# A two-layer attention block on one NeuronCore: filling work dealt out over three units of the next branch, a new order ahead of the attention, and gated outputs on GpSimd

## The reference, cut to what matters

```python
def merge_branches(o_m, o_s, o_a, z_m, z_s, z_a, g, lw):
    y_m = (o_m.reshape(B, T, MLA_WIDTH) * jax.nn.silu(z_m)) @ lw['w_o_mla']
    y_s = (o_s.reshape(B, T, SWA_WIDTH) * jax.nn.silu(z_s)) @ lw['w_o_swa']
    y_a = (o_a.reshape(B, T, AX_WIDTH) * jax.nn.silu(z_a)) @ lw['w_o_ax']
    y = jax.nn.sigmoid(g_m) * y_m + jax.nn.sigmoid(g_s) * y_s + jax.nn.sigmoid(g_a) * y_a
    return y @ lw['w_out']

def hybrid_layer(x, ctx, c, c_ctx, lw, pos, update_ctx):
    ...
    h = rmsnorm(x, lw['norm_w']) * (1 + scale) + shift
    p = h @ lw['w_in']
    k_m, v_m, k_s, v_s, k_a, v_a = project_kv(p[..., :KV_COLS], lw, pos)
    q_m, q_s, q_a, z_m, z_s, z_a, g = project_q(p[..., KV_COLS:], lw, pos)
    ...
    x = x + gate * merge_branches(o_m, o_s, o_a, z_m, z_s, z_a, g, lw)
```

## Time and profile before

| what | us |
|---|---|
| runs, median (lowest to highest) | 1764.51 (1763.14 to 1766.87) |
| the profiled execution, its own time | 1766.55 |
| its span | 1764.7 |
| PE busy | 1694.5 (96%) |
| PE weight loads busy | 1488.8 (84%) |
| DVE busy | 1081.5 (61%) |
| ACT busy | 1047.0 (59%) |
| POOL busy | 535.6 (30%) |
| mean granted clock of PE | 0.98 |

### The profile page before, as it was taken

The page is one execution under the profiler, slowest core; times in us unless marked ns, Lnnn a source line. Parts: engine busy times, 40 slices in busy tenths (PEclk is TensorE's granted clock), DMA queues, the critical chain, the costliest instruction groups (busy, mean ns, idle before and its releaser), DMA issues.

```text
span 1764.7 us, 26891 instructions
## 1 busy us (share of the span) xinstructions
PE 1694.5 (96%) x10496; PEld 1488.8 (84%) x10496; DVE 1081.5 (61%) x2188; ACT 1047.0 (59%) x1919; POOL 535.6 (30%) x306
## 2 busy tenths in 40 slices
PE   7999999999999999999999998999999999999997
PEld 3778888889989889899889986788888887888787
DVE  6534777765555656665774655567775656665634
ACT  3345777766666777765321254577766678777322
POOL 2432223222132211222322354333233333233442
PEclk8999999999999999999999999999999999999999
DMA  9111111111121111111635231112122221222642
GB/s 330 40 37 29 26 46 37 48 31 49 44 60 37 43 43 43 37 43 42 230 123 191 97 99 49 41 38 56 40 53 66 72 72 31 62 59 55 203 144 95
DMA packets 178530, 129.51 MB, mean 73 GB/s; under 512 B 21658, under 2 KB 167652, under 8 KB 178404
## 3 DMA queue, kind: packets, MB, share of 16 engines
q1 hardware_dynamic: 174240, 115.36, 22.8%
q10 hardware_dynamic: 2884, 8.24, 1.2%
q0 software_dynamic: 1280, 4.20, 0.7%
HBM read 123.58 MB, written 4.19 MB: 72 GB/s over the span
## 4 chain that ended last, share of the span: by engine, by line
PE 76%; DVE 10%; ACT 8%; issue 3%; POOL 2%; DMA 1%; SPq 0%; DVEq 0%; ACTq 0%; POOLq 0%
PE acc L1383 55%; PE wide L1435 6%; PE ptp L1455 6%; PE pv L1468 4%; PE pv L1469 3%; DVE nmax L2019 2%; ACT e L1702 2%; DVE pt L2044 1%; ACT w_hi L1620 1%; POOL h_lo L1871 1%; POOL w_lo L1826 1%; DVE k_s L1572 1%; DVE k_m L1572 1%; ACT k_m L1563 1%; DMA w_raw<-in_ada_w 1%
## 5 line engine op out<-in xcount | busy, mean ns | idle before, releaser
L1826 POOL TENSOR_TENSOR w_lo<-w_raw,w_hi 128x1024 fp32r<-128x1024 f32 (+2 forms) x192 | 392.5, 2047 | 1042.5 <-ACT w_hi L1620 1042.5
L1383 PE MATMUL acc<-h_hi,w_hi 128*128 128x512 f32 (+2 forms) x1320 | 465.5, 353 | 12.0 <-DVE cq_lo L1574 3.9
L1383 PE MATMUL acc<-h_hi,w_lo 128*128 128x512 f32 (+2 forms) x1320 | 463.9, 352 | 0.0
L1383 PE MATMUL acc<-h_lo,w_hi 128*128 128x512 f32 (+2 forms) x1320 | 458.7, 351 | 0.3 <-POOL h_lo L1871 0.3
L1383 PEld LDWEIGHTS acc<-h_hi,w_hi 128*128 128x128 f32 (+1 forms) x1320 | 249.6, 189 | 52.8 <-issue 8.9
L2019 DVE TENSOR_REDUCE nmax<-wide 128x1 f32<-128x768 f32 (+3 forms) x240 | 189.6, 790 | 170.4 <-PE wide L1435 168.8
L1717 ACT ACTIVATE pt<-ptp 128x512 fp32r<-128x512 f32 (+3 forms) x312 | 165.7, 563 | 213.2 <-PE ptp L1455 211.5
L1383 PEld LDWEIGHTS acc<-h_hi,w_lo 128*128 128x128 f32 (+1 forms) x1320 | 249.3, 189 | 33.4
L1383 PEld LDWEIGHTS acc<-h_lo,w_hi 128*128 128x128 f32 (+1 forms) x1320 | 246.6, 188 | 34.4 <-POOL h_lo L1871 0.5
L1709 ACT ACTIVATE e<-e,einv 128x768 f32<-128x768 f32 (+3 forms) x240 | 193.4, 806 | 68.1 <-DVE einv L2036 67.7
L2044 DVE TENSOR_TENSOR pt<-ptp,pt 128x512 fp32r<-128x512 f32 (+3 forms) x312 | 191.9, 640 | 44.4 <-ACT pt L1717 44.4
(11 more groups left out here) (217 smaller groups left out, 3074.7 us busy)
## 6 DMA issues: line engine op xcount, KB each, us to landing
w_raw<-in_w_in SPq DMA_DIRECT2D x102, 512.0 KB, 3.9
w_raw<-in_ada_w SPq DMA_DIRECT2D x48, 512.0 KB, 5.1
w_raw<-in_w_out SPq DMA_DIRECT2D x16, 512.0 KB, 3.8
w_raw<-in_w_in SPq DMA_DIRECT2D x16, 256.0 KB, 3.1
w_raw<-in_w_o_mla SPq DMA_DIRECT2D x16, 256.0 KB, 2.7
w_raw<-in_w_o_swa SPq DMA_DIRECT2D x16, 256.0 KB, 2.8
w_raw<-in_w_o_ax SPq DMA_DIRECT2D x16, 256.0 KB, 2.7
w_raw<-in_mla_w_uq SPq DMA_DIRECT2D x16, 144.0 KB, 2.3
```

The lines of the kernel that those rows point to most:

```text
L1383: ins = nc.tensor.matmul(dst, lhs, rhs, start=first, stop=last)
L1826: nc.gpsimd.tensor_tensor(w_lo[s][:, 0:k], w_raw[s][:, 0:k], f(w_hi[s][:, 0:k]), ALU.subtract).then_inc(w_lo_ready, 1)
```

## The change

It has seven parts.

1. `BEHIND = 3`: the filling work of a branch is dealt out over its units and three of the next branch. The first branch counts three units more, the last three fewer, and the branch for `fill` is that of unit i-3.
2. `ak`'s first group is deferred: its event `E` comes after row tile 1 is turned and modulated, not before.
3. The second `latent_sums` (context) comes before the query latents, not between them.
4. `KC` comes in `first_pair` behind the second group of values, and the groups there stand in another order; the z groups name another `oldest` chunk, which decides how soon later weights may be split.
5. The gating at `O` moves from DVE (a product with the factor 0.5) to POOL (a plain product, with waits for POOL's own earlier writes); the factor goes into the pieces `H` and `L` of og.
6. In `y` (for the second and third branch) and `wout`, DVE writes the product back into the PSUM bank and not to SBUF, and adds from there. A group that follows in this bank waits for the sum (`th_done`, `xr_done`) and not for the product.
7. swa's sum of the exponentials with the sink, one column, is a `tensor_scalar` with a column as scalar and not a `tensor_tensor`.

```diff
-DRAIN = 2
+DRAIN, BEHIND = 2, 3
...
-        left[BRANCHES[-1]] += DRAIN
+        left[BRANCHES[0]] += BEHIND
+        left[BRANCHES[-1]] += DRAIN - BEHIND
...
             if i < len(units) + DRAIN:
-                branch = u["branch"] if u else BRANCHES[-1]
+                branch = units[min(max(i - BEHIND, 0), len(units) - 1)]["branch"]
...
-        ak = project("ak", l, ck, "x", roped=True, oldest=ck, low_last=True, halves=True, parts=2)["steps"]
+        ak_x = project("ak", l, ck, "x", roped=True, oldest=ck, low_last=True, halves=True, parts=2, defer=True)
+        ak = ak_x["steps"]
         ckv = project("ckv", l, cks[0], "x", t=0, oldest=ck, halves=True, parts=2)["steps"]
         run_all([ak[0], ckv[0]])
         turn_rows(0)
         modulate_rows(0)
         run_all(ak[1:])
-        ropes_ak = n["rope"]
         turn_rows(1)
         modulate_rows(1)
+        ak_x["read"]()
+        ropes_ak = n["rope"]
         run_all(ckv[1:])
...
         latent_sums("x")
+        latent_sums("c")
         query_latents(0, "c")
         query_latents(1, "x")
-        latent_sums("c")
         query_latents(1, "c")
...
-        emit("KC", l_done=n["l"])
+        ropes_read = n["l"]
...
-            order = [keys_["x"], q0["x"], values[0], keys_["c"], q1["x"], values[1]]
-            order += [q0["c"], z["c"], q1["c"], z["x"]] if "c" in tgs else [z["x"]]
+            order = [keys_["x"], q0["x"], values[0], q1["x"], values[1], keys_["c"]]
+            order += [z["c"], q0["c"], q1["c"], z["x"]] if "c" in tgs else [z["x"]]
             for g in order:
                 go(g)
+                if g is values[1]:
+                    emit("KC", l_done=ropes_read)
...
-                        if before is not None and before["dve"] and before["kind"] not in ("statb", "statq"):
+                        if before is not None and before["kind"] == "wout":
+                            if new(xr_done, before["xr"]):
+                                pe.wait_ge(xr_done, before["xr"])
+                        elif before is not None and "th" in before:
+                            if new(th_done, before["th"]):
+                                pe.wait_ge(th_done, before["th"])
+                        elif before is not None and before["dve"] and before["kind"] not in ("statb", "statq"):
...
+                elif ev == "O":
+                    if new(o_sum, pa["o"] + 1):
+                        pool.wait_ge(o_sum, pa["o"] + 1)
...
+                    nc.gpsimd.tensor_tensor(o, o_half[own, 0:k], o, ALU.mult).then_inc(o_free, 1)
...
-                            nc.vector.scalar_tensor_tensor(t, t, 1.0, src[:, 0:N], ALU.add, ALU.mult).then_inc(acc_free, 1)
+                            nc.vector.scalar_tensor_tensor(src[:, 0:N], t, 1.0, src[:, 0:N], ALU.add, ALU.mult).then_inc(acc_free, 1)
...
-                            nc.vector.tensor_tensor(y, y, t, ALU.add).then_inc(th_done, 1)
+                            nc.vector.tensor_tensor(y, src[:, 0:N], y, ALU.add).then_inc(th_done, 1)
...
-                        nc.vector.tensor_tensor(x_add[:, :], src[:, 0:256], gate[:, s, c], ALU.mult).then_inc(acc_free, 1)
+                        nc.vector.tensor_tensor(src[:, 0:256], src[:, 0:256], gate[:, s, c], ALU.mult).then_inc(acc_free, 1)
...
-                        link(nc.vector.tensor_tensor(esink[:, r:r + 1], esink[:, r:r + 1], esum[:, r:r + 1], ALU.add))
+                        link(nc.vector.tensor_scalar(esink[:, r:r + 1], esum[:, r:r + 1], esink[:, r:r + 1], None, ALU.add))
...
-                    nc.vector.scalar_tensor_tensor(o, o_half[own, 0:k], 0.5, o, ALU.mult, ALU.mult).then_inc(o_free, 1)
```

More of the change, by code:

```diff
@@ L732, in first_pair @@
                               needs=lambda: latents, what="qm", head=1, **roped(tg)) for tg in tgs}
-            z = {tg: project("z", l, cz, tg, branch=BRANCHES[0], t=1, before_z=0, oldest=cq) for tg in tgs}
-            order = [keys_["x"], q0["x"], values[0], keys_["c"], q1["x"], values[1]]
-            order += [q0["c"], z["c"], q1["c"], z["x"]] if "c" in tgs else [z["x"]]
+            z = {tg: project("z", l, cz, tg, branch=BRANCHES[0], t=1, before_z=0, oldest=None if tg == "x" else c) for tg in tgs}
+            order = [keys_["x"], q0["x"], values[0], q1["x"], values[1], keys_["c"]]
+            order += [z["c"], q0["c"], q1["c"], z["x"]] if "c" in tgs else [z["x"]]
             for g in order:
                 go(g)
+                if g is values[1]:
+                    emit("KC", l_done=ropes_read)
             zs[BRANCHES[0], 1] = [z[tg] for tg in tgs]
@@ L997, in build @@
               for i in part]
-    a_row, x_add = shared("a_row", [4, D], F, 83968), shared("x_add", [P, 256], F, 49152)
+    a_row = shared("a_row", [4, D], F, 83968)
     xres = shared("xres", [P, TT, D], F, 100352)
@@ L1673, in _ @@
                             act.wait_ge(acc_done, g["acc"])
-                        ins = high_parts(*pieces(g, e["kv"]))
+                        hi, _, whole_o = pieces(g)[0][0]
+                        ins = nc.scalar.activation(hi, whole_o, ACT.Copy, scale=0.5)
                     elif g["kind"] == "kx":
@@ L1815, in _ @@
             new = counting()
-            link = splits = tiles = 0
+            link = splits = tiles = ropes = 0
             for e in events:
@@ L1858, in _ @@
                     link += 1
+                    ropes = g["rope"]
                     nc.gpsimd.tensor_tensor(swapped[rows, :], swapped[rows, :], sin[rows, :], ALU.mult).then_inc(rope_link, 1)
@@ L1865, in _ @@
                             pool.wait_ge(rope_done, g["rope"])
+                elif ev == "O":
+                    pa = e["pa"]
+                    own, _ = o_rows(pa)
+                    k = len(pa["units"]) * P
+                    if new(o_sum, pa["o"] + 1):
+                        pool.wait_ge(o_sum, pa["o"] + 1)
+                    if new(acc_free, pa["zs"]):
+                        pool.wait_ge(acc_free, pa["zs"])
+                    if new(w_lo_ready, splits):
+                        pool.wait_ge(w_lo_ready, splits)
+                    if new(rope_done, ropes):
+                        pool.wait_ge(rope_done, ropes)
+                    o = o_t[own, pa["h"] // 2, o_tokens(pa)]
+                    nc.gpsimd.tensor_tensor(o, o_half[own, 0:k], o, ALU.mult).then_inc(o_free, 1)
+                    if new(o_free, pa["o"] + 1):
+                        pool.wait_ge(o_free, pa["o"] + 1)
                 elif ev == "XM":
@@ L1999, in _ @@
                         x = xres[:, g["tt"], c]
-                        nc.vector.tensor_tensor(x, x, x_add[:, :], ALU.add).then_inc(xr_done, 1)
+                        nc.vector.tensor_tensor(x, src[:, 0:256], x, ALU.add).then_inc(xr_done, 1)
                 elif ev == "L":
@@ L2007, in _ @@
                         ins = nc.vector.scalar_tensor_tensor(y_lo[:, g["t"], c], y2[:, g["t"], c], 0.5, f(y_hi[:, g["t"], c]), ALU.mult, ALU.subtract)
+                    elif g["kind"] == "og":
+                        hi, lo, whole_o = pieces(g)[0][0]
+                        ins = nc.vector.scalar_tensor_tensor(lo, whole_o, 0.5, f(hi), ALU.mult, ALU.subtract)
                     else:
```

## The result

| | us |
|---|---|
| before, median (lowest to highest) | 1764.12 (1763.14 to 1766.87) |
| changed, median (lowest to highest) | 1778.69 (1772.46 to 1779.37) |
| ratio, 95% interval | 1.0075 (1.0062 to 1.0089) |
| forecast | 1757, range 1746 to 1767 |

The range missed by 12 us and the sign was wrong. The profiled execution took 1778.86 us, its span is 1777.1.

A forecast was written before the change was run, and what follows sets the result against it. PE was taken as the bound, 96% busy: its work, its waits and the slow clock behind them. Terms of 22.3 us off and 15.0 on gave 7.3 us less, from 1764.51 to 1757 us, range 1746 to 1767.

The forecast's parts named there:

- The two handovers of layer 1 get mla's and swa's own leftovers until the closing: Part 1, layer 1's branch handovers: filling removes waits of 2.5 and 3.0 us and slow clock, 9.5 us off.
- Its price is thinner filling in mla: Part 1, mla of both layers: less filling per unit becomes PE waiting, 4 us on, bounds 1 and 9.
- nothing there: Part 1, layer 0's handovers: filling already stands in every step, so no gain was counted.
- The handover to ax: Part 1, layer 1 at 1461 to 1467 us: the 3.0 us wait and 3.4 us of slow clock go.
- Parts 3 and 4: Latent sums, key copy and first pair's order, ahead of the attention: 2.3 and 5.4 us off.
- Part 7: swa's column sum: never above 217 ns, the wait near 372.5 us shrinks, 3.1 us off, bounds 0 and 4.
- Part 6: Sums out of PSUM: 0.5 us gained, 4.5 us lost as 11 groups in layer 0 wait for the bank.
- Part 2: ak deferred: second ckv tile waits 2.9 us in each layer, less h_lo waits, plus slow clock; 6.5 us on.
- Part 5: Gating on POOL instead of DVE: 1.5 us off, bounds -5 and 6.
- DVE's relief: Rival, mla: less DVE work shortens the way to PV, some 8 us more off, 1749 us; 17%.
- hold up the weights: Rival: gating on POOL makes w_lo late and PE waits; 1772 us with 20 of 120 passes; 9%.
- It comes out even: Rival: nothing may run at the handovers, or new waits bring twice the slow clock; 1764 us; 16%.

The follow-up runs named there:

- a_mla3: Changed kernel with the three units behind at the end of mla only, swa's filling over its own units: 1775.88 us, ratio 1.0064.
- a_swa3: Changed kernel with the three units behind at the end of swa only: 1757.67 us, ratio 0.9958.
- e_half: Changed kernel with part 1 undone, but mla's heads 0 to 3 thinned and the later heads making up for it: 1774.05 us, ratio 1.0056.
- e_late: Changed kernel with three units behind mla only, heads 0 to 3 dealt full and the second half thin: 1772.71 us, ratio 1.0045.
- b_esink: Kernel before with part 7 alone: 1759.11 us, ratio 0.9970.
- nb_ak: Changed kernel with parts 1 and 2 undone: 1757.45 us, ratio 0.9949.
- b_gate: Kernel before with part 5 alone, the gating on POOL: 1764.06 us, ratio 1.0003.

## Why the prediction was wrong

The step that failed is "The two handovers of layer 1 get mla's and swa's own leftovers until the closing", with "Its price is thinner filling in mla" at 4 us. In its place the runs show work for swa's first head made late and key pieces moved in front of `o_half`: 17 us for three units behind mla (a_mla3), nothing for three behind swa (a_swa3). Its sum was -9.5 + 4.0; part 1 measured +17 alone and +19 in the changed kernel. All other parts together were forecast at -1.8 and measured -5.6 (0.9968, with -3.5 to -7.8 by its interval). The miss is part 1 alone, and in it the units behind mla. By its steps:

- **That leftovers exist.** True for swa, false for mla. Each item that counts for mla in `queue` is used by mla or by swa's first head: its queries and keys at the first scores, its values at the first `PV`. `SA` and `PV` force them however little credit there is. I took the name in `of` for the branch that pays and did not ask who reads the item first. The list says it: `item((SWA, 0), "mla", ...)`. The empty place of layer 1 was filled all the same, because swa's own items start three units later and last until the outputs close. In exchange there is a burst ahead of swa's first scores in layer 1, two thin steps behind them, and PE waits up to 6.5 us for the query pieces, in one layer or both. The turn of layer 1 went from 6.3 us of idle time to 7.3, and to 5.2 with part 1 undone.
- **Layer 0's handovers: "nothing there".** There was nothing to gain, but something to lose: 8.6 us, more than in layer 1. A stretch without a wait was costed at nothing, though its cover was the 7.7 us by which the queries were early: now PE waits 2.9 us there, at a clock of 0.66 over 10 us.
- **4 us for thinner units.** In the changed kernel heads 0 to 3 lose 10.2 us and heads 4 to 6 give back 2.1, 8 in all, inside the bound of 9. But e_half, thin units alone, costs some 15 us, outside it, so the term was mis-sized as well, and how the 17 us divide between thinness and lateness stays open: e_half's 15 and e_late's 14 do not add up to them. The amount is not the cause alone. Filling comes in parts of some 0.9 us, so that 0.12 us less a unit means one part less in about every eighth unit, and from there on every other part stands in another step. Where such a step has few parts, or its pieces fill DVE, and it meets the close of a pass, PE waits: up to 2.1 us for `o_half` in the changed kernel, 4.4 in e_half and e_late. One, two and three units cost 16, 30 and 17 us.
- **The handover to ax.** The wait of 3.0 us and its slow clock are gone, as forecast; a wait of 2.7 us for a z reading and 0.83 over 10 us took its place.
- **Parts 3 and 4** were right: -7.7 forecast, -7.4 measured, with the wait for key pieces as forecast.
- **Part 7** was right in kind, short in size (-3.1 against -5.3, interval 3.0 to 7.6, bound 4). I counted one wait, where ten of the 80 sums took 0.4 us or more. By the same reckoning b_esink's trace has 2.9 us less idle time in layer 0's turn, where that wait lies, but also 1.2 us less in layer 1's turn and 1.7 in swa behind it.
- **Part 6**: +4.0 net forecast, +4.9 measured, with eight of the eleven waits in the list. The rule of the Trainium skill on a PSUM source (VectorE: DVE Perf Modes, The TRN2 errata), 62 cycles more than for one in SBUF, is not borne out here: the sum with its source in PSUM takes 0.69 us as it did from SBUF. DVE of the changed kernel at 709 us:

```profile
709.01 0.69 DVE L2000 SCALAR_TENSOR_TENSOR acc<-th_x,acc 128x512 f32<-128x512 f32 x1
709.73 0.69 DVE L2003 TENSOR_TENSOR y<-acc,y 128x512 f32<-128x512 f32 x1
```

- **Part 2**: the waits came as forecast, 2.5 us in the list (2.7 from the starts) against 2.9, in both layers. The chain of the forecast adds up to 60.4 us and not 60.6 (57.9 + 0.63 + 0.57 + 1.3), which gives 2.6 us of wait, as measured. The cost is nearer 3.4 than 6.5, since the waits net of `h_lo` were 2.5 us and not 3.1, and in the kernel that nb_ak is compared with the clock fell behind one of the two and not both (by the starts of the matmuls, 1.3 us of slow clock where 3.4 were counted).
- **Part 5**: -1.5 forecast, 0 measured, inside its error.
- **The rivals.** DVE's relief carried nowhere: in b_gate, 50 us less of it left mla's waits as they were (4.9 and 4.0 us in layer 0, against 4.4 and 3.9). POOL did not hold up the weights: PE's matmuls wait 2.8 us in all for `w_lo` in b_gate and in the kernel before. "It comes out even" came nearest, yet its mechanism (nothing may run at the handovers) gives 0, not a loss. No rival had the loss that came: an item needed soon made later. The range was too narrow on the slow side besides. The slow bounds of the terms, taken by squares, give 11 us and the fast ones 8, not some 7 to either side; 1778.7 would lie outside that as well.

What stays open: which step each jump with one and two units behind comes from was read in two places only (the key pieces before `o_half`, the late query pieces). That a change of the credit alone moves waits some 400 us later is shown by e_half (thinned up to 245 us, idle time in ax from 587 us on); a rule that would say beforehand where they fall is not. The 3.4 us of part 2 are uncertain by their interval.

## What to carry to other kernels

Before work is put off, find the first reader of every item in the queue, not the branch that it is booked on: what the next stage reads first is not slack. A stretch without waits has a lead (here 7.7 us between a query piece and its use), and a change that touches its order must be costed against that lead. Where filling comes in lumps beside a chain that closes every second step, a small change of the rate moves all lumps behind it; its effect can't be had from an average per step, so try two or three neighbouring rates before you believe one.

## What was not expected of the hardware

120 products of 64x256 moved from DVE to POOL took 50 us off the one (1081.5 to 1031.3) and put 92 us on the other (535.6 to 627.7, b_gate), and the time stayed within 0.03% in two comparisons of three (the changed kernel with the products on DVE is 0.2% slower, the intervals overlapping). One column sum, 80 times 159 ns at the median, was worth 5.3 us, since ten of them took 0.4 to 2.2 us, the one at 372.5 us beside a POOL instruction of 2.9 us. And around a wait of 2.9 us of PE the clock was 0.66 over 10 us, so that the clock took up to as much again as the wait.
